# Router products among the output projections, the norm's scale put on afterwards, and the sample tokens as one 128-column stationary operand

## The reference, cut to what matters

```python
xn = rmsnorm(x, norm_mix_g);  z = xn @ w_in          # 10248 columns: q,k / v / o / gates / u / gv / mq / branch gates
... # mLSTM (needs v), chunked gMLP (needs gv), memory attention
mixed = g0 * br_mlstm + g1 * br_gmlp + g2 * br_mem
x = x + mixed @ w_out                                # the output projection
h = rmsnorm(x, norm_moe_g)                           # rsqrt(mean(x*x) + eps) per row, times a gain per column
p_group = softmax(h @ w_router_group + b);  grp = top1(p_group)
e_logits = h @ w_router_expert + b;  top 2 of the 8 experts in the group
for e in range(32):                                  # 1024 -> 256 -> 1024 each
    hidden = silu(h @ w_g[e]) * (h @ w_u[e]);  y += combine[:, e] * (hidden @ w_d[e])
```

## Time and profile before

| | |
|---|---|
| median of 3 runs | 923.2 us (922.76 to 926.06) |
| profiled execution, own time | 923.59 us |
| its span | 921.9 us |
| TensorE busy, mean granted clock | 870.8 us (94%), 0.979 |
| VectorE, ScalarE, GpSimd busy | 602.4, 483.2, 47.6 us |
| DMA | 182.91 MB, mean 198 GB/s |

### The profile page before, as it was taken

How to read it: one execution, slowest core, us unless ns; L and a number is a source line. 1 busy time by engine, 2 the same in 40 slices (tenths; PEclk the granted TensorE clock), 3 DMA queues, 4 the chain that set the end, 5 groups by cost and what they waited for, 6 DMA issues and landing times.

```text
span 921.9 us, 13063 instructions
## 1 busy us (share of the span) xinstructions
PE 870.8 (94%) x5259; PEld 781.0 (85%) x5259; DVE 602.4 (65%) x806; ACT 483.2 (52%) x609; POOL 47.6 (5%) x109
## 2 busy tenths in 40 slices
PE   5999999989999999999999998599999999999994
PEld 5888998879989999999999997387787887887882
DVE  4564467762345446496565456837789899889875
ACT  5564456653333234443333434556767767767753
POOL 3302001110011011000000000000000000000000
PEclk9999999999999999999999999689999999999998
DMA  9746433333447557744444473029999999999961
GB/s 261 239 141 228 148 105 103 103 114 95 137 84 166 129 91 155 177 138 149 138 137 141 150 276 119 1 96 352 325 348 346 353 351 360 350 341 351 350 226 60
DMA packets 99234, 182.91 MB, mean 198 GB/s; under 512 B 5384, under 2 KB 71168, under 8 KB 99168
## 3 DMA queue, kind: packets, MB, share of 16 engines
q1 hardware_dynamic: 95264, 171.47, 57.2%
q0 software_dynamic: 3104, 8.37, 3.5%
q10 hardware_dynamic: 800, 2.18, 0.9%
HBM read 176.17 MB, written 5.82 MB: 197 GB/s over the span
## 4 chain that ended last, share of the span: by engine, by line
PE 75%; DVE 9%; DMA 6%; ACT 6%; issue 3%; SPq 1%; ACTq 0%; DVEq 0%
PE pj L527 38%; PE pj L786 15%; PE pj L808 8%; DMA arena<-in_w_exp_up 3%; PE pj L571 2%; ACT unit_r L884 2%; DVE unit_r L1224 1%; DMA arena<-in_w_exp_down 1%; DMA arena<-in_w_mem_v 1%; DVE w_r L1233 1%; PE ms L825 1%; ACT w_r L895 1%; PE ms L655 1%; DMA arena<-in_w_mem_k 1%; PE ms L751 1%
## 5 line engine op out<-in xcount | busy, mean ns | idle before, releaser
L1224 DVE TENSOR_TENSOR unit_r<-arena,unit_r 128x2048 fp32r<-128x2048 f32 x63 | 144.4, 2292 | 187.4 <-ACT unit_r L884 182.6
L1233 DVE TENSOR_TENSOR w_r<-arena,w_r 128x2048 fp32r<-128x2048 f32 x96 | 218.9, 2289 | 49.3 <-ACT w_r L895 48.7
L527 PE MATMUL pj<-xn_r,unit_r 128*128 128x320 f32 x1536 | 235.0, 311 | 0.0
L527 PEld LDWEIGHTS pj<-xn_r,unit_r 128*128 128x128 f32 x1536 | 225.6, 188 | 5.7 <-issue 2.8
L895 ACT ACTIVATE w_r<-arena 128x2048 fp32r<-128x2048 f32 x96 | 183.8, 1917 | 50.9 <-DMA arena<-in_w_exp_up 33.6
L786 PE MATMUL pj<-w_r,xg 128*128 128x512 f32 x768 | 192.2, 400 | 0.0
L786 PEld LDWEIGHTS pj<-w_r,xg 128*128 128x128 f32 x768 | 143.0, 190 | 30.9
L884 ACT ACTIVATE unit_r<-arena 128x2048 fp32r<-128x2048 f32 x63 | 120.2, 1908 | 33.0 <-PE pj L527 12.0
L808 PE MATMUL pj<-w_r,hidT 128*128 128x512 f32 x384 | 93.3, 392 | 4.4 <-DVE hidT L1563 3.0
L808 PEld LDWEIGHTS pj<-w_r,hidT 128*128 128x128 f32 x384 | 71.5, 188 | 22.1 <-DVE w_r L1233 5.8
L527 PE MATMUL pj<-unit_r,xn_r 128*128 128x256 f32 (+1 forms) x576 | 70.0, 282 | 0.0
(11 more groups left out here) (329 smaller groups left out, 749.1 us busy)
## 6 DMA issues: line engine op xcount, KB each, us to landing
arena<-in_w_in SPq DMA_DIRECT2D x40, 1024.0 KB, 5.2
arena<-in_w_exp_gate SPq DMA_DIRECT2D x64, 512.0 KB, 4.5
arena<-in_w_exp_up SPq DMA_DIRECT2D x64, 512.0 KB, 5.8
arena<-in_w_exp_down SPq DMA_DIRECT2D x64, 512.0 KB, 5.1
arena<-in_w_mem_k SPq DMA_DIRECT2D x4, 1024.0 KB, 7.3
arena<-in_w_mem_v SPq DMA_DIRECT2D x4, 1024.0 KB, 6.5
arena<-in_w_br_mem SPq DMA_DIRECT2D x4, 1024.0 KB, 7.7
arena<-in_w_br_mlstm SPq DMA_DIRECT2D x4, 1024.0 KB, 5.1
```

The costliest lines, as they stand in the source:

```text
L527: last = mm(bank_of(s)[0:out_rows, 0:out_cols], l, r, start=k == 0, stop=k == len(pairs) - 1)
L1224: v.tensor_tensor(unit_r[n % RING][:, 1, :], ringw[:, n % RING, :], unit_r[n % RING][:, 0, :], ALU.subtract).then_inc(u_lo, 1)
L1233: v.tensor_tensor(w_r[u % NS][:, 1, :], raw_w[u % NS], w_r[u % NS][:, 0, :], ALU.subtract).then_inc(m_lo, 1)
```

## The change

Four edits, made together:

1. *Sample tokens.* GpSimd copies the high and the rest of the 64 sample tokens side by side into a tile of 128 columns (`pair_samples`; for `v`, `gv` and `res`). `project_samples` then needs 8 x 2 = 16 matmuls per step in place of 24: both parts times the weight's high, both times its rest. Rows 0 to 63 of the bank hold the high part's sum and rows 64 to 127 the rest's, and the evacuation adds both: for `v` and `gv` ScalarE copies the upper rows and VectorE adds the lower (for `gv` the gelu comes afterwards, `sample_gelu`), for `res` VectorE adds twice.
2. *Scale afterwards.* The rows go to the router as x times the gain, without 1/sqrt. Each output projection's 256 columns are multiplied by the gain as soon as they are added, and squared in quarters on ScalarE. The logits are scaled per token after they come back from the transpose, and so are the expert weights; the silu takes the scale of its slot (`comb` has two more columns per group).
3. *Router among the projections.* The transposes `hnT` go chunk by chunk (3 per chunk) and the eight router products `logits` stand between the steps `res` of the next unit; only the chunks 6 and 7 come after the last one. They have a ring of their own, `hx` (3 banks of `ms`), and the fourth bank collects the logits. `ranks` is 3 matmuls, the totals are a step of their own, and `gather` does the eight high chunks first and waits for each one-hot matrix by itself. The last unit's tiles come in the order 2, 0, 1. The splitting of the rows (`hn_high`, `hn_rest`) is cut at 96 of 128 columns, so that the most of it can go before the last unit ends.
4. *Expert loads.* SyncE loads the first expert unit after dense unit 55 of 64 and the second after unit 61; the slots have other places. The fifth waits for the last projection.

```diff
@@ make_steps
     for u in range(4):
         n = unit("w_out", u * 256)
-        for i in range(3):
-            step("res", u, i, ring="pj", eng="D", unit=n, last=i == 2)
+        for j, i in enumerate(RES_ORDER[u]):
+            step("res", u, i, ring="pj", eng="D", unit=n, last=j == 2, place=j)
+            if u and j < 2:
+                for c in (2 * u - 2, 2 * u - 1):
+                    if j == 0:
+                        step("hnT", c, ring="hx", eng="AD"[c % 2])
+                    else:
+                        step("logits", c, ring=None, eng=None)
+    step("hnT", 6, ring="hx", eng="A")
+    step("hnT", 7, ring="hx", eng="D")
     step("moe_norm", ring=None, eng=None)
...
@@ sync
+                if n == len(UNITS) - 9:
+                    load_unit(0, 0)
+                elif n == len(UNITS) - 3:
+                    load_unit(0, 1)
@@ tensor
+            def project_samples(s, x_s, w):
+                for k in range(KC):
+                    for q in range(2):
+                        last = mm(bank_of(s)[:, 0:256], x_s[:, k, :, :], w[:, q, k, :], start=k + q == 0, stop=k == KC - 1 and q == 1)
+                return last
...
+                elif kind == "hnT":
+                    c, = a
+                    for j, i in enumerate(RES_ORDER[c // 2]):
+                        pe.wait_ge(s_xs, 3 + 3 * (c // 2) + j + 1)
+                        last = tr(b[:, t0:t0 + n], xs_tm[0:n, i, c * 128:(c + 1) * 128], ident[0:n, 0:n])
+                if kind == "logits":
+                    pe.wait_ge(*done("hnT", c))
+                    last = mm(ms[:, 3, 0:T], wrow[:, c * (G + E):c * (G + E) + 128], hnT[:, c, :], start=c == 0, stop=c == KC - 1)
@@ scalar, step res (k counts the twelve steps)
+                    if k in (1, 4):
+                        unit_high(0, k // 4)
...
+                        hn_high(i, 0, 96)
+                    act.wait_ge(*done("res", u, i))
+                    af(junk[0:n, :], x_tm[0:n, i, u * 256:(u + 1) * 256], ACT.Square, accum_out=sq[0:n, i, u:u + 1]).then_inc(s_ss, 1)
@@ vector, step res
+                    if i == 2:
+                        link(v.tensor_tensor(x_, x_, b[TS:2 * TS, 0:256], ALU.add))
+                    v.tensor_tensor(x_, x_, b[0:n, 0:256], ALU.add).then_inc(free, 1)
+                    v.tensor_tensor(xs_tm[0:n, i, cs], x_tm[0:n, i, cs], gm_g[0:n, cs], ALU.mult).then_inc(s_xs, 1)
+                    if (u, i) == (0, 1):
+                        unit_rest(0, 0)
+                    elif (u, i) == (1, 1):
+                        unit_rest(0, 1)
@@ gpsimd
+            def pair_samples(dst, x_r):
+                for part in range(2):
+                    g.tensor_copy(dst[:, :, part, :], x_r[:, part, :, TP:T]).then_inc(s_pair, 1)
```

More of the change, by code:

```diff
@@ L118, in make_steps @@
         for i in range(3):
-            step("v", u, i, ring="pj", eng="A", unit=n, last=i == 2)
+            step("v", u, i, ring="pj", eng="AAD"[i], unit=n, last=i == 2)
         if u == 1:
@@ L158, in make_steps @@
         for i in range(3):
-            step("gv", u, i, ring="pj", eng="A", unit=n, last=i == 2)
+            step("gv", u, i, ring="pj", eng="AAD"[i], unit=n, last=i == 2)
             if u >= 1:
@@ L171, in make_steps @@
         n = unit("w_out", u * 256)
-        for i in range(3):
-            step("res", u, i, ring="pj", eng="D", unit=n, last=i == 2)
-    step("moe_norm", ring=None, eng=None)
[L175 to L180, removed]
+        for j, i in enumerate(RES_ORDER[u]):
[8 more added lines that the diff above has]
+    step("hnT", 7, ring="hx", eng="D")
+    step("moe_norm", ring=None, eng=None)
+    step("logits", 6, ring=None, eng=None)
+    step("logits", 7, ring=None, eng=None)
+    step("lgt", ring="hx")
+    step("ranks", ring="hx")
+    step("totals", ring="hx")
     return steps, units
 STEPS, UNITS = make_steps()
-NBANK = {"pj": 4, "ms": 4}
-_seen = {("pj", "A"): 0, ("pj", "D"): 0, ("ms", "A"): 0, ("ms", "D"): 0}
-_ring_steps = {"pj": [], "ms": []}
+NBANK = {"pj": 4, "ms": 4, "hx": 3}
+_seen = {("pj", "A"): 0, ("pj", "D"): 0, ("ms", "A"): 0, ("ms", "D"): 0, ("hx", "A"): 0, ("hx", "D"): 0}
+_ring_steps = {"pj": [], "ms": [], "hx": []}
 _by_name = {}
@@ new lines, in _ @@
+                    if u == 3 and s["place"] < 2:
+                        hn_rest(i, 0, 96, s["place"] + 1)
+                elif kind == "hnT" and a[0] % 2:
+                    c, = a
+                    v.tensor_copy(hnT[:, c, :], b[:, 0:T]).then_inc(free, 1)
+                elif kind == "moe_norm":
+                    dve.wait_ge(s_ss, 5 + 12)
+                    link(v.tensor_reduce(ssx[:, 20:23], sq[:, :, :], axis=AX.X, op=ALU.add))
+                    v.tensor_scalar(var[:, 20:23], ssx[:, 20:23], 1.0 / D, EPS, ALU.mult, ALU.add).then_inc(s_var, 1)
+                    refine(5, 20, 23)
@@ L1734, in _ @@
                         load_state(h + 2)
+                elif kind == "res" and a == (3, 2):
+                    pool.wait_ge(ready["pj"], _by_name["res", 2, 2]["at"] + 1)
+                    g.memset(hn_h[64:128, 2, :, :].bitcast(FP32), 0.0).then_inc(s_hnz, 1)
+                    pool.wait_ge(u_lo, len(UNITS))
+                    g.memset(hn_l[64:128, 2, :, :].bitcast(FP32), 0.0).then_inc(s_hnz, 1)
                 elif kind == "u" and a[0] == 7:
```

337 lines of the change are left out of this document (201 added, 136 removed).

## The result

The changed kernel took 912.09 us (median of 4 runs, 910.83 to 915.11) beside 924.63 us for the kernel before: ratio 0.9856, 95% interval 0.9816 to 0.9897. A second measurement, taken beside the experiments, gave 0.9832 (0.980 to 0.9864), 907.71 us beside 922.11. So it is faster by 1.4% and 1.7%: 13 and 15 us by the ratios, 12.5 and 14.4 us by the medians. The forecast was 12.9 us and 910.7 us. The profiled execution took 910.83 us, its span is 909.0 us.

What follows compares the result with a forecast made beforehand. TensorE was taken to bound the kernel, 94% busy, with DMA also full among the experts. Gains of 3.2 (v), 1.5 (gv) and 8.2 us (projections to first expert) sum to 12.9: 923.6 to 910.7 us, range 902 to 919.

Steps and rivals of the forecast that it cites:

- v: Sample tokens in steps v: 16 matmuls in place of 24 gain 0.81 us per step, 3.2 us for four steps.
- the third pair (for res): GpSimd copies for the output projections: one could hold TensorE 0.7 us; left out of the sum as over in time.
- gv: Sample tokens in steps gv: 3.2 us saved less a 1.7 us wait for GpSimd's copies, net 1.5 us.
- rival D: Clock falls during the projections because TensorE waits about a fifth of that stretch: slower, 934 us; chance 0.05.
- Projections to first expert: First output projection to first expert, router products between projections: 69.3 us against 77.5, gain 8.2, with 6.8 us of waits.
- The clock there: From projections to first expert: clock expected low again for gather, with little TensorE work from 45 to 53 us.
- Experts: Expert stage starts when gather is over and keeps its length, so what comes ahead shifts it whole: 0 us.
- a sign that it was wrong: Expert stage changing its length by over 2 us was named as showing the prediction wrong.
- Expert loads: First two expert loads issued among the dense loads: price 0, removing only ScalarE's wait, which cost TensorE 0.35 us.
- A: Projections: the waits aren't there, they take 36.5 us and the gain is 6.8 us more, 904 us; chance 0.16.
- B: Projections: waits twice as long through handovers of 0.2 us between three engines, 6.8 us longer, 917.5 us; chance 0.16.
- C: Same time: doubled projection waits and the pair of gv held until 362 us (1.8 more), 919.3 us; chance 0.07.

Runs made afterwards that it cites:

- loads_back: Changed kernel with the first two expert loads issued behind the last dense load, as before: 918.78 us, ratio 0.9938.
- the six: Six profiles of kernels with pairs in gv and the outputs of n: the changed kernel twice, late splits, 19 unread matmuls, expert loads moved back, early copies for gv.
- unpaired: Changed kernel with the sample tokens of v and gv as before (24 matmuls, no GpSimd copies), output projections still paired: 912.09 us, ratio 0.9893.
- no_n: Changed kernel without the eight outputs of the normalizer n, which are left unwritten: 904.78 us, ratio 0.9796.
- after: The changed kernel with all four edits, first profile: 912.09 us against the kernel before, ratio 0.9856.
- after_again: The changed kernel with no further edit, second profile: 907.71 us, ratio 0.9832.
- early_pair: Changed kernel with GpSimd's copies for gv made behind the third head's outputs instead of the fourth's: 907.0 us, ratio 0.9834.
- before: The kernel before the change, unedited: 924.63 us in the first measurement, 922.11 us in the second.
- before_no_n: Kernel before the change without the outputs of the normalizer n, left unwritten: 920.73 us, ratio 0.9999.
- the late splits: Changed kernel with the splits of the first two expert units made behind the splitting of the rows: 905.54 us, ratio 0.9813.

## Why the prediction was right, point by point

**v, 3.2 us: right.** The unit after the first takes 7.68 us in place of 8.49. Ten profiles with pairs have 34.1 to 35.8 us for 21 to 25, four without 38.0 to 39.1. The copies on GpSimd fitted, as the sum had it, and those of the third pair (for res) were over in time as well: no step res waited for them.

**gv, 1.5 us: the mechanism right, the sum too good.** The two copies took 1.18 us together, the price taken from the earlier trace rows, and VectorE didn't lengthen them. In the second profile the wait was 1.68 us, the forecast's 1.7. But GpSimd's outputs came up to 1.8 us later in other executions, and in three of five the clock fell behind the wait, a cost of 1.7 us that I had priced for the projections (rival D) and not here. The five profiles with late copies give 78.92 us in the mean against 78.98: no gain, where 1.5 was forecast. The term that was mis-sized is the wait: I took the time of GpSimd's last outputs from the kernel before and gave it no spread, and the clock behind the wait no price. Without the outputs of n both are gone and the whole 3.2 us come. The Trainium skill ("TensorE: Matmul & The Clock Gate", HAM oscillation) has the clock fall where bursts alternate with waits; the runs agree for three of the five waits in gv (1.8, 2.4 and 3.4 us) and for the 9.8 us of loads_back, and speak against it for the waits of up to 1.6 us in the projections.

**What no step had: the stall behind the first head's outputs.** 1.4 us in the mean of the six. Over all dense units from 21 to 61 the five profiles with outputs of n and late copies are 2.3 us shorter than the four unpaired ones (339.1 against 341.4), where 4.7 was forecast; no_n, at 335.6, is another 3.6 us shorter.

**Projections to first expert, 8.2 us: 9.8 came.** 67.4 to 67.8 us in five profiles (after, after_again, unpaired, early_pair, no_n), against 77.5 and 77.3 in before and before_no_n. The terms erred in opposite senses. The waits were 1.5, 1.6, 0.7 and 0.2, 4.0 us against 6.8: the places were those that I had named, and the splits were the cause of the first three, but the third and fourth were small. That each wait of TensorE lets ScalarE and VectorE catch up would explain it; that is argued, not shown. Without waits the projections take 38.2 and not 36.5 us (with the late splits they took 38.4): a projection behind transposes took 3.11 and not 2.88, a pair of transposes 1.08 and not 0.8. So the last projection ended after 42.2 us (43.3 forecast), and from there gather's start took 8.9 (9.1), gather and slot weights 16.7 (16.9).

**The clock there:** 1.00 in the projections, low for gather. Rival D falls for this kernel; loads_back shows its mechanism, behind a wait of 9.8 us.

**Experts, 0:** 297.8 us before and 294.2 after, from the first expert to the last matmul, looks like a gain of 3.6; but the three forms of the kernel before had 297.8, 296.6 and 294.3, the eleven of the changed one 294.0 to 297.8. So it is spread between executions, most likely of the loads (not shown). The prediction had named a change of over 2 us there as a sign that it was wrong; the spread alone is larger than that, so the sign was no test.

**Expert loads, 0: wrong as an account.** Nothing was lost by where they went, as forecast; but I took them for a part without effect. Without them the reordering of the projections would have brought 2 us and not 9.8.

**Rivals.** A (no waits) didn't come by itself; the late splits made it, 64.1. B and C didn't come.

**How much of the hit is luck.** The mechanism of v and of the last stretch was right. That the sum met the measured time so closely is luck: too much in the dense part (2.4) stood beside too little in the last (1.6) and the spread of the start (the high part of unit 21 came between 194.4 and 200.0 us over all profiles), which no step moves. In the two profiles that the forecast spoke of, the 12.9 us of span are a loss of 0.3 up to the first projection (a gain of 4.7 was forecast), a gain of 9.7 from there to the first expert (8.2), and 3.5 behind it (0), which is the spread just named.

## What to carry to other kernels

Price a transfer's place by who stands behind its consumer in the new order, not by what it cost in the old one. Look for transfers of single elements: their cost shows at whatever shares the DMA engines with them, and can be nothing in one order of the program and some us in another. A wait before full work costs its length, and sometimes a fall of the clock behind it.

## What the runs showed of the hardware

- The outputs of n (stores of 4-byte elements) slow the DMA beside them: a load of 1 MB landed in 18.4 us in place of 5.2. From 262 to 300 us packets of 1 KB took 77 to 132 ns and packets of 4 KB 428 to 694 ns in the mean (nine profiles with these outputs); without them 51 to 52 and 168 to 183 ns (five profiles). It is a tail that does it: the median packet of 1 KB takes 46 ns in all fourteen, the longest 6.0 to 9.3 us with the outputs and 0.6 to 0.8 us without. The Trainium skill ("DMA: Bandwidth & Descriptors", Specifications) has transfers under 512 B done as read-modify-write; rows of 512 B in place of elements took the slowness away, which agrees, but no run shows that this is the cause.
- TensorE's instructions come in packets of 16 KB on queue 8, 43 of them for 0.70 MB, most of them in 1 us (that they are TensorE's is inferred from the count). The Trainium skill ("Advanced Engine Details and Errata", ISA Cache) gives 16 KB as 256 instructions; 10,314 records of TensorE over 256 are 40, which agrees roughly. When a packet took 8 us, ScalarE learned of a tile that had ended at 270.4 us only at 277.45, and TensorE stood 1.6 us.
- The clock fell at waits of 1.8, 2.4, 3.4 and 9.8 us, and did not at 1.7 and 0.9 in gv or at 1.5 and 1.6 in the projections. The 1.8 and the 1.7 are 1.77 and 1.68 us: so close a pair with opposite ends says that the length of the wait alone doesn't decide. With the same matmuls at the same distances the clock stayed up through one gather and fell 1.5 us into another.
